# Three pairs of consecutive dense layers, each pair in one block, with the second layer's input split chunk by chunk into buffers of its own

## What is computed

```
# block 1, end of the parallel mixers (gated DeltaNet beside a convolution)
y = sigmoid(gate_a) * (o_gdn @ w_gdn_out) + y_conv_gated    # dense layer gdn_out
x = layer_norm(ALPHA * x + y @ w_mix_out)                   # dense layer mix_out
# ... cross attention on a memory of 256 tokens, a feed-forward layer ...
# block 2, end, and block 3, beginning
x = x + y2 @ w_out_2                                        # dense layer out_2
h = x @ w_in_3                                              # layers qk_3, v_3, rest_3
# ... neighbourhood attention (adds a bias table), latent attention ...
merged = sigmoid(g_a) * (y_a @ w_branch_na) + sigmoid(g_b) * (y_b @ w_branch_mla)   # branches_3
x = layer_norm(ALPHA * x + merged @ w_out_3)                # dense layer out_3
```

## Time and profile before

| | us |
|---|---|
| median of 3 runs | 3190.18 |
| lowest and highest run | 3188.05, 3190.51 |
| the profiled execution | 3194.44 |
| its span in the trace | 3192.7 |
| PE busy in it | 2924.4 (92%) |
| DVE, ACT, POOL busy | 1034.9, 1019.8, 1162.7 |

### The profile page before, as it was taken

How to read it: one execution, slowest core, us unless ns; L and a number is a source line. 1 busy time by engine, 2 the same in 40 slices (tenths; PEclk the granted TensorE clock), 3 DMA queues, 4 the chain that set the end, 5 groups by cost and what they waited for, 6 DMA issues and landing times. The chain is left out here.

```text
span 3192.7 us, 35648 instructions
## 1 busy us (share of the span) xinstructions
PE 2924.4 (92%) x14270; PEld 2282.5 (71%) x14270; DVE 1034.9 (32%) x1727; ACT 1019.8 (32%) x1439; POOL 1162.7 (36%) x379
## 2 busy tenths in 40 slices
PE   8999999999989988889999899877899789999998
PEld 6887788886688767668878587344787436678876
DVE  2110216997334431431110300555300635431101
ACT  3331222234444223233321322244122444143312
POOL 4443443444363346144444442100344011444442
PEclk9999999999999999999999899877999889999999
DMA  4222231243100233122222124000223001122221
GB/s 153 104 92 92 79 119 66 100 144 125 67 1 28 106 119 119 40 79 92 92 95 103 42 103 160 33 3 1 83 102 125 1 24 40 66 92 92 98 87 66
DMA packets 40847, 258.01 MB, mean 81 GB/s; under 512 B 4128, under 2 KB 5536, under 8 KB 13088
## 3 DMA queue, kind: packets, MB, share of 16 engines
q1 hardware_dynamic: 37136, 248.09, 21.9%
q10 hardware_dynamic: 3600, 8.39, 0.7%
HBM read 243.88 MB, written 12.58 MB: 80 GB/s over the span
## 5 line engine op out<-in xcount | busy, mean ns | idle before, releaser
L207 POOL TENSOR_TENSOR weights_lo<-weights_raw,weights_hi 128x2048 fp32r<-128x2048 f32 x201 | 940.8, 4681 | 1567.5 <-ACT weights_hi L198 1567.5
L228 PE MATMUL psum<-x_hi,weights_hi 128*128 128x512 f32 (+1 forms) x2560 | 1009.3, 394 | 100.3 <-DVE x_lo L331 54.5
L229 PE MATMUL psum<-x_lo,weights_hi 128*128 128x512 f32 (+1 forms) x2560 | 1003.0, 392 | 0.0
L230 PE MATMUL psum<-x_hi,weights_lo 128*128 128x512 f32 (+1 forms) x2560 | 1002.2, 391 | 0.0
L198 ACT ACTIVATE weights_hi<-weights_raw 128x2048 fp32r<-128x2048 f32 x202 | 386.6, 1914 | 833.3 <-PE psum L230 725.8
L228 PEld LDWEIGHTS psum<-x_hi,weights_hi 128*128 128x128 f32 x2560 | 489.3, 191 | 217.8 <-issue 84.9
L230 PEld LDWEIGHTS psum<-x_hi,weights_lo 128*128 128x128 f32 x2560 | 489.1, 191 | 100.9
L229 PEld LDWEIGHTS psum<-x_lo,weights_hi 128*128 128x128 f32 x2560 | 489.8, 191 | 98.9
L377 DVE SCALAR_TENSOR_TENSOR arena<-arena,psum 128x512 f32<-128x512 f32 x66 | 45.4, 688 | 554.8 <-PE psum L230 554.8
L228 PE MATMUL psum<-h_hi,weights_hi 128*128 (+1 forms) x528 | 207.7, 393 | 7.7 <-PEq L342 7.7
L229 PE MATMUL psum<-h_lo,weights_hi 128*128 (+1 forms) x528 | 207.2, 392 | 0.0
(11 more groups left out here) (258 smaller groups left out, 3068.1 us busy)
## 6 DMA issues: line engine op xcount, KB each, us to landing
weights_raw<-in_stream SPq DMA_DIRECT2D x202, 1024.0 KB, 4.8
keep_gates<-arena ACTq DMA_DIRECT2D x24, 256.0 KB, 2.0
arena<-keep_gates SPq DMA_DIRECT2D x3, 2048.0 KB, 9.6
arena<-in_na_bias SPq DMA_DIRECT2D x1, 3584.0 KB, 12.9
arena<-in_x_t SPq DMA_DIRECT2D x2, 1024.0 KB, 8.0
keep_x<-arena ACTq DMA_DIRECT2D x1, 2048.0 KB, 8.5
keep_yc<-arena SPq DMA_DIRECT2D x1, 2048.0 KB, 7.0
arena<-keep_yc SPq DMA_DIRECT2D x1, 2048.0 KB, 14.0
```

Source lines behind the costliest of these rows:

```text
L207: K.nc.gpsimd.tensor_tensor(K.wlo[:, 1 - slot, :, :], K.raw[:, 1 - slot, :, :], K.whi[:, 1 - slot, :, :].bitcast(F32), ALU.subtract).then_ ...
L228: K.nc.tensor.matmul(out, whi, xhi, start=start, stop=False)
L229: K.nc.tensor.matmul(out, whi, xlo, start=False, stop=False)
L230: return K.nc.tensor.matmul(out, wlo, xhi, start=False, stop=stop)
```

## The change

Each pair becomes one block: `phase_gdn_mix` (8 tiles), `in_3` with `out_2` in front (20 tiles), and `phase_branches_out` (8 tiles). Six views `rounded_u` over arena units are added as split buffers, so that the second layer's halves don't take the place of the first's. DVE splits each chunk of the second layer's input right after it is finished (`split_ready`), PE starts the second layer with its first tile peeled and waits for each chunk (`y_split`). The loads that stood at the second block's beginning (`keep_x`, `mem_t`) and at the end of `in_3` (`na_bias`) are issued at the beginning of the joint block, ahead of its weight tiles.

```
+        self.rounded = {u: place(f"rounded_{u}", [P, KC, T], F32R, at + u * T * 4) for u in (12, 24, 32, 36, 44)}
...
-def stream_pe(K, pe, name, n=T, t0=0, split=False):
+def stream_pe(K, pe, name, n=T, t0=0, split=False, x=None, ready="x_split"):
-    xhi, xlo = K.xhi, K.xlo
+    xhi, xlo = x or (K.xhi, K.xlo)
...
-            pe.wait_ge(K.s("x_split").sem, K.s("x_split").at(k + 1))
+            pe.wait_ge(K.s(ready).sem, K.s(ready).at(k + 1))
...
+def split_ready(K, dve, c, unit, x, ready, n):
+    hi, lo = x
+    done, split = K.s("y_hi_done"), K.s("y_split")
+    dve.wait_ge(ready.sem, ready.at(n))
+    K.nc.vector.tensor_copy(hi[:, c, :], K.A[:, unit, :]).then_inc(done.sem, done.n())
+    dve.wait_ge(done.sem, done.at(c + 1))
+    K.nc.vector.tensor_tensor(lo[:, c, :], K.A[:, unit, :], hi[:, c, :].bitcast(F32), ALU.subtract).then_inc(
+        split.sem, split.n())
...
-def phase_gdn_out(K):
+def phase_gdn_mix(K):
+    y = K.rounded[36], K.rounded[24]
...
         sp.dma_start(K.A[:, 16:24, :], K.dram["keep_yc"]).then_inc(s("reloaded").sem, s("reloaded").n(16))
+        sp.dma_start(K.A[:, 0:8, :], K.dram["keep_x"]).then_inc(s("x_back").sem, s("x_back").n(16))
+        sp.dma_start(K.A[:, 48:56, 0:N_MEM], K.dram["mem_t"]).then_inc(s("mem_in").sem, 16)
+    def load_next(sp):
+        sp.wait_ge(s("mem_in").sem, 16)
+    def pe(pe):
+        stream_pe(K, pe, "gdn_out", split=True)
+        stream_pe(K, pe, "mix_out", t0=4, split=True, x=y, ready="y_split")
...
+            split_ready(K, dve, c, 8 + c, y, s("y_ready"), c + 1)
...
-    phase_residual(K, "out_2", 8, reload=False, alpha=1.0, stats=False)
...
-def phase_branches_3(K):
+def phase_branches_out(K):
+    y = K.rounded[44], K.rounded[12]
...
+        pe.wait_ge(s("branch_taken").sem, s("branch_taken").at(12))
+        stream_pe(K, pe, "out_3", split=True, x=y, ready="y_split")
...
-                nc.vector.tensor_tensor(A[:, c - 8, :], A[:, c - 8, :], A[:, c, :], ALU.add)
+                nc.vector.tensor_tensor(A[:, c - 8, :], A[:, c - 8, :], A[:, c, :], ALU.add).then_inc(
+                    s("y_ready").sem, s("y_ready").n())
+                split_ready(K, dve, c - 32, c - 8, y, s("y_ready"), c - 31)
...
-    names = ["qk_3", "v_3", "rest_3"]
+    names = ["out_2", "qk_3", "v_3", "rest_3"]
+    mixed = K.rounded[24], K.rounded[32]
+        stream_pe(K, pe, "out_2", split=True, x=mixed)
+        stream_pe(K, pe, "qk_3", t0=4, split=True, ready="y_split")
...
+            nc.vector.scalar_tensor_tensor(A[:, c, :], A[:, c, :], 1.0, K.ps[:, 2 * slot + j, :], ALU.mult,
+                                           ALU.add).then_inc(*free_bank(K, j))
+            split_ready(K, dve, c, c, (K.xhi, K.xlo), s(f"bank_free_{j}"), t + 1)
...
-    phase_stream(K, "in_3", names, pe=pe, act=act, presplit=0, load_next=load_bias)
+    phase_stream(K, "in_3", names, pe=pe, act=act, dve=dve, presplit=8, presplit_to=mixed, load=load_bias, load_next=wait_bias)
```

More of the change, by code:

```diff
@@ L595, in _ @@
             if presplit is not None:
[L596 removed]
+                split_chunks(K, dve_, presplit, width=width, x=presplit_to)
             if norm:
@@ L1381, in dve @@
                 s("y_ready").sem, s("y_ready").n())
-    phase_stream(K, "gdn_out", "gdn_out", dve=dve, load=load, presplit=24)
+            split_ready(K, dve, c, 8 + c, y, s("y_ready"), c + 1)
+    phase_stream(K, "gdn_mix", ["gdn_out", "mix_out"], pe=pe, dve=dve, load=load, load_next=load_next, presplit=24, stats=LayerNorm(
+        K, 0, lambda eng, c: eng.wait_ge(s(f"bank_free_{c % 2}").sem, s(f"bank_free_{c % 2}").at(c // 2 + 5)),
+        K.A[:, 32:36, :]))
 def phase_residual(K, label, presplit, reload=True, alpha=ALPHA, stats=True, load_more=None):
@@ L1416, in block1_mixers @@
     phase_gdn_scan(K)
[L1417 to L1422, removed]
+    phase_gdn_mix(K)
 def stream_pe_tokens(K, pe, names, n_tok=NT, t0=0):
@@ L2321, in pe @@
                     last.then_inc(K.s(("first_done", "tile_done")[m // 2]).sem, 1)
+        pe.wait_ge(s("branch_taken").sem, s("branch_taken").at(12))
+        stream_pe(K, pe, "out_3", split=True, x=y, ready="y_split")
     def dve(dve, t, g, slot):
+        if t == 0:
+            dve.wait_ge(s("x_split").sem, s("x_split").at(KC))
+        if t >= 4:
+            for j in range(2):
+                c = 2 * (t - 4) + j
+                wait_bank(K, dve, g, j)
+                nc.vector.scalar_tensor_tensor(A[:, c, :], A[:, c, :], ALPHA, K.ps[:, 2 * slot + j, :], ALU.mult,
+                                               ALU.add).then_inc(*free_bank(K, j))
+            return
         for m in range(4):
@@ L2337, in block3, with dve @@
     A = K.A
-    names = ["qk_3", "v_3", "rest_3"]
+    names = ["out_2", "qk_3", "v_3", "rest_3"]
+    mixed = K.rounded[24], K.rounded[32]
     def pe(pe):
-        stream_pe(K, pe, "qk_3", split=True)
-        stream_pe_tokens(K, pe, "v_3", t0=4)
-        stream_pe(K, pe, "rest_3", t0=6)
+        stream_pe(K, pe, "out_2", split=True, x=mixed)
+        stream_pe(K, pe, "qk_3", t0=4, split=True, ready="y_split")
+        stream_pe_tokens(K, pe, "v_3", t0=8)
+        stream_pe(K, pe, "rest_3", t0=10)
+    def dve(dve, t, g, slot):
+        if t >= 4:
+            return
+        for j in range(2):
+            c = 2 * t + j
+            wait_bank(K, dve, g, j)
+            nc.vector.scalar_tensor_tensor(A[:, c, :], A[:, c, :], 1.0, K.ps[:, 2 * slot + j, :], ALU.mult,
+                                           ALU.add).then_inc(*free_bank(K, j))
+            split_ready(K, dve, c, c, (K.xhi, K.xlo), s(f"bank_free_{j}"), t + 1)
     def act(act, t, g, slot):
+        t -= 4
+        if t < 0:
+            return
         for j in range(2):
```

28 lines of the change are left out of this document (19 added, 9 removed).

## The result

| kernel | median us | runs | ratio to the kernel before |
|---|---|---|---|
| before, beside it | 3190.04 | 16 | |
| changed | 3176.94 | 16 | 0.9959 (0.9950 to 0.9968) |

The change takes 13.1 us off, the interval is 10.2 to 16.0. The forecast was 3172.8 us, 4.1 us lower than the median, with 17.4 us off. The profiled execution of the changed kernel took 3173.86 us, 3.1 us less than its median.

A forecast was written before the change was run, and what follows sets the result against it. PE, busy 92% of the 3192.7 us span, was taken as the bound. Removing 27.3 us and adding 4.6, 2.0 and 3.3 gave 17.4 off: 3190.2 to 3172.8 us, range 3163.5 to 3180.5 for 8 in 10.

The forecast's parts named there:

- Joints 1 and 2 closed: Between gdn_out and mix_out, and out_2 and in_3: the whole cost of 9.84 and 9.16 us goes, nothing replacing it on DVE.
- the last chunk held until T + 7.4: Second layer's chunk 7, T being the last result: even if POOL's split holds DVE, it precedes PE's need at T + 9.3.
- The late weight tile: gdn_out's block: 3.15 MB of loads ahead delay its first weight tile 8.1 us; PE stands 4.6 us, upper price 7.3.
- the clock's loss: PE's lower clock in the 8 us after its new wait in gdn_out's block: 2.0 us lost, ends 0 and 2.6.
- the rival that the tile passes them in the queue: gdn_out's weight tile served beside keep_x, so the terms of 4.6 and 2.0 go: 3166.2 us, chance 0.15.
- DVE's chain in joint 3: branches_3 into out_3: POOL's split holds chunk 5's subtraction; PE stands 0.9, 1.2 and 1.2 us, 3.3 together.
- the rival by the Trainium skill's section on psum-queue depth-cycling: At out_3, three small gaps also lower the clock, 2.6 us more: 3180.4, within the larger-loss rival of chance 0.2.
- The bias table at nothing: Bias table ahead of out_2's first weight tile costs nothing: tile lands at 2251.7, ACT wants it at 2252.38.
- The hold by issue order: At out_3, of two-input DVE and reading POOL instructions the second to issue blocks: POOL at 2734.3 wins against 2734.6.
- The joint costs: The three layer boundaries cost 9.84, 9.16 and 8.32 us in the profiled execution, 27.3 us to come off.
- The sum -27.3 + 4.6 + 2.0 + 3.3 = -17.4: Whole kernel: three boundary costs removed, weight-tile wait, lower clock and DVE's chain added, against the profiled span of 3192.7: 3175.3.
- so I carry the difference over to it: Whole kernel: the 17.4 us from the profiled execution is taken off the median too, 3190.2 to 3172.8 us.

## Why the prediction was right, and where its size was off

**Joints 1 and 2 closed: right.** 16.32 and 16.31 us from take to take, 16.32 forecast. The split of the last chunk came 2.6 us after the last result, as worked out (1127.04 to 1129.64), and POOL's split, which began 0.14 us behind that subtraction (1129.09, and by the same 0.14 us in every trace with joint 1 closed), held nothing. So the case that the prediction allows for, the last chunk held until T + 7.4, did not come up.

**The late weight tile: right in place and in size.** ACT's split was 8.0 us later in its block than before (22.92 against 14.93), 8.1 forecast, from 388 GB/s (it came at 1096.76, not 1093.1, since the pair itself began 3.8 us later in this execution, at 1071.93 instead of 1068.15); PE's stand was 4.4 us (4.6), the clock's loss 1.7 (2.0). 3.15 MB in 8.0 us is 393 GB/s. With the loads moved the stand went, which rules out the rival that the tile passes them in the queue. By the 358 GB/s that the Trainium skill gives as an estimate (SBUF — State Buffer, Summary: rules for kernel authors) it would have been 8.8 us; the trace disagrees.

**DVE's chain in joint 3: right.** One subtraction of chunk 5 held for 5 us, by POOL's split that began just before it, and three stands. They sum to 2.2 us, 3.3 forecast; with what lies around them 3.1 us of the joint's cost are left, so 5.2 are won, where the sum had 5.0. That the two nearly meet is partly luck: the stands were 1.1 us shorter than forecast, and the 0.3 us that each cost beyond its idle time were not in the sum. The clock was 1.00 from 2717 to 2738, so these three gaps of up to 0.9 us did not lower it; the rival by the Trainium skill's section on psum-queue depth-cycling (TensorE: Matmul & The Clock Gate) found nothing here.

**The bias table at nothing: right.** ACT's split of the tile behind it, at 2248.61 in the new trace, still waited for PE (14.55 us), not for the DMA.

**The hold by issue order: right.** The 4.77 us CAST, which the prediction names beside the rule for two SBUF inputs, has one such input. The sum of 1.60 us in the earlier trace rows and the subtraction of 4.98 us here have two, and each began behind POOL's split and ended some 0.5 us after it.

**The joint costs: mis-sized.** The sum -27.3 + 4.6 + 2.0 + 3.3 = -17.4 holds for the profiled executions: the pairs' stretches fell by 3.5 + 8.9 + 5.9 = 18.3 us. The step that failed is "so I carry the difference over to it", from the one profiled execution to the median. The 9.84 and 9.16 us of joints 1 and 2 were each the dear one of two outcomes. In the four traces in which pair 1 has the old code it is dear in two (91.30, 91.29) and cheap in two (88.48, 88.43); pair 2 is dear in three (90.79, 90.59, 90.82) and cheap in one (87.88). So by this estimate a mean execution has 2.9 / 2 + 2.9 / 4 = 2.2 us less to win, which makes the forecast 15.2 us off instead of 17.4. The measured 13.1 (10.2 to 16.0) and 17.5 (13.1 to 22.0) lie about that. That the profiled execution stood 4.3 us over the median was the hint: part of it was these outcomes (the second trace of the kernel before is 6.9 us shorter, 3.6 of it in the three pairs). Four traces are few, and the remaining 2 us are within what the measurement can tell; whether anything else is in them stays open.

Of the 20.6 us between the two spans the other 2.3 lie in the rest of the program, which moves by some us between executions. The medians are 13.1 us apart and not 20.6, since the profiled execution of before stood 4.4 us over the median of the 16 and that of the changed kernel 3.1 us under its own. For the latter no trace shows a cause.

## What to carry to other kernels

Splitting the next layer's input chunk by chunk closed a joint of 6 to 10 us, but only as far as everything queued for the second layer was not put in front of the first one's weight stream: 3 MB ahead of a weight tile cost 6.4 us of the 9.8 won. Before moving work off an engine that is held, ask by whom it is held: POOL's weight split held DVE's 0.4 us CAST for 4.8 us at the start of four blocks of the changed kernel, and one wait on POOL gave another 9 to 14 us, nearly as much as the whole change. And a stall read from one trace needs a second execution of the same code before its size goes into a sum.

## What the runs showed of the hardware

A stand of PE of the same length, 3.28 us in the same place, was followed by 12 matmuls at full clock in one execution and by a clock of 0.63 in another, with the fall 0.5 us after PE had started again. With the first stand alone (POOL's wait in the kernel before; 3.28 and 2.55 us) the clock stayed full behind joints 1 and 2. So the cost of two stands near each other is not the sum of what each costs alone: where the first lowers the clock, the second is shorter.

A DVE instruction that arrived 0.2 us behind POOL's split was held to its end (4.98 us from 2720.58, POOL from 2720.39), so order decides down to 0.2 us. At joint 1 of the same trace DVE's subtraction began 0.14 us ahead of POOL's split (1128.95 against 1129.09) and took its usual 0.69; there POOL's split took 5.00 us instead of 4.6. The hold is for DVE's instructions on SBUF alone. The products that read PSUM beside SBUF were not held: inside one split of POOL in branches_3 a product took 0.68 us, and the sum right behind it, with both inputs in SBUF, 4.38 (timelines of DVE, then POOL, of the changed kernel).

```profile
2709.97 0.68 DVE L2367 TENSOR_TENSOR arena<-arena,psum 128x512 f32<-128x512 f32 x1
2710.68 4.38 DVE L2371 TENSOR_TENSOR arena<-arena 128x512 f32<-128x512 f32 x1
```

```profile
2709.51 5.00 POOL L208 TENSOR_TENSOR weights_lo<-weights_raw,weights_hi 128x2048 fp32r<-128x2048 f32 x1 [6.29 <-ACT weights_hi L199]
```
